# One-hots of the first block by a comparison on VectorE instead of three steps on ScalarE

## The reference, cut to what matters

```
scores = einsum('bshpd,hpnd->bshpn', q, sub_keys)
sv, si = top_k(scores, 16)                     # 16 best keys of each half
tv, tp = top_k(sv0 + sv1, 16)                  # 16 best of the 256 pairs
eidx   = si0 * 128 + si1                       # expert number, at tp
gw     = softmax(tv)
a      = gelu(einsum('td,ted->te', x, expert_u[eidx])) * gw
out    = einsum('te,ted->td', a, expert_v[eidx])
```

## Time and profile before

| | us |
|---|---|
| median of 3 runs (lowest, highest) | 3220.09 (3214.86, 3222.01) |
| the profiled execution | 3220.44 |
| its span | 3218.6 |
| VectorE busy in it | 2066.2 |
| TensorE matmuls busy | 2748.8 |
| ScalarE busy | 616.2 |
| DMA moved | 951.25 MB, mean 296 GB/s |

### The profile page before, as it was taken

The page is one execution under the profiler, slowest core; times in us unless marked ns, Lnnn a source line. Parts: engine busy times, 40 slices in busy tenths (PEclk is TensorE's granted clock), DMA queues, the critical chain, the costliest instruction groups (busy, mean ns, idle before and its releaser), DMA issues.

```text
span 3218.6 us, 31451 instructions
## 1 busy us (share of the span) xinstructions
PE 2748.8 (85%) x12106; PEld 2196.4 (68%) x12106; DVE 2066.2 (64%) x2764; ACT 616.2 (19%) x1230; POOL 912.3 (28%) x724
## 2 busy tenths in 40 slices
PE   5899889798999989989999999655657766999997
PEld 4688768587888868866888888554656665444443
DVE  6879675637355346822625116999999879656667
ACT  1011131020011010011110002011147778200000
POOL 0110001101010000000100002467776667656664
PEclk9999999899999989977999999877777776899998
DMA  9994359838885623321987446999999998999998
GB/s 363 390 399 137 104 188 380 358 131 345 355 357 221 254 86 128 106 68 39 393 324 307 148 158 270 391 367 415 421 421 410 387 388 266 351 401 414 415 413 354
DMA packets 149156, 951.25 MB, mean 296 GB/s; under 512 B 16560, under 2 KB 16560, under 8 KB 52400
## 3 DMA queue, kind: packets, MB, share of 16 engines
q0 software_dynamic: 103680, 620.80, 48.1%
q1 hardware_dynamic: 44208, 320.65, 26.3%
q10 hardware_dynamic: 1152, 8.26, 0.7%
HBM read 945.45 MB, written 4.19 MB: 295 GB/s over the span
## 4 chain that ended last, share of the span: by engine, by line
PE 42%; DVE 22%; DMA 21%; ACT 6%; issue 5%; POOL 4%; DVEq 0%; ACTq 0%; POOLq 0%
PE G L438 33%; DMA acc<-v_rows,proj 7%; DMA aring<-ada 7%; DVE aring L1276 3%; DVE vec L1868 3%; DMA mix<-v_rows,proj 3%; DVE aring L1840 2%; ACT vec L1139 2%; PE M L831 2%; DVE ring L1840 2%; DVE proj L1357 2%; DVE proj L1527 1%; POOL acc L426 1%; PE G L819 1%; DMA vec<-peer_u,proj 1%
## 5 line engine op out<-in xcount | busy, mean ns | idle before, releaser
L438 PE MATMUL G<-h,ring 128*128 128x256 f32 x4928 | 1081.9, 382 | 13.2 <-ACT h L915 13.2
L438 PEld LDWEIGHTS G<-h,ring 128*128 128x128 f32 x4928 | 942.9, 192 | 146.4 <-issue 16.5
L401 POOL DMA_DIRECT2D aring<-ada x208 | 109.8, 529 | 1633.7 <-DVE mods L1276 1626.4
L1276 DVE CUSTOM_DVE_ANT_0 aring<-aring,acc,vec 128x2048 f32<-128x2048 f32 x176 | 411.0, 2351 | 181.4 <-DMA aring<-ada 180.6
L438 PE MATMUL G<-proj,ring 128*128 128x256 f32 x2080 | 462.1, 386 | 10.6 <-DVE proj L1633 4.8
L438 PEld LDWEIGHTS G<-proj,ring 128*128 128x128 f32 x2080 | 403.0, 194 | 69.9 <-issue 12.8
L416 POOL DMA_INDIRECT aring<-peer_u,proj x128 | 217.5, 1700 | 348.6 <-DVE proj L1806 223.0
L872 PE MATMUL M<-sq,mix 128*128 128x512 f32 x688 | 301.5, 596 | 1.1 <-ACT mix L1153 1.1
L1840 DVE CUSTOM_DVE_ANT_0 aring<-sq,aring 128x2048 f32<-128x2048 f32 x108 | 245.4, 2291 | 27.6 <-DMA aring<-peer_u,proj 17.1
L1868 DVE SCALAR_TENSOR_TENSOR vec<-acc,dots,vec 128x1024 f32<-128x1024 f32 x149 | 191.2, 1283 | 100.9 <-DMA acc<-v_rows,proj 93.5
L883 ACT ACTIVATE proj<-G 128x256 f32 (+1 forms) x170 | 65.2, 383 | 979.2 <-PE G L438 979.1
(11 more groups left out here) (325 smaller groups left out, 2829.7 us busy)
## 6 DMA issues: line engine op xcount, KB each, us to landing
ring<-weights SPq DMA_DIRECT2D x219, 1024.0 KB, 5.0
aring<-ada POOLq DMA_DIRECT2D x208, 1024.0 KB, 12.2
sq<-v_blocks SPq DMA_DIRECT2D x43, 1024.0 KB
proj<-v_blocks SPq DMA_DIRECT2D x21, 1024.0 KB
ring<-first SPq DMA_DIRECT2D x16, 896.0 KB, 8.1
acc<-v_rows,proj POOLq DMA_INDIRECT x151
x<-xT SPq DMA_DIRECT2D x1, 2048.0 KB, 12.2
acc<-conds ACTq DMA_DIRECT2D x2, 1024.0 KB, 11.1
```

The costliest lines, as they stand in the source:

```text
L401: pool.dma_start(aring[:, n % SLOTS, :], ada[a]).then_inc(ada_in[n % SLOTS], 16)
L438: mm = nc.tensor.matmul(bank[:, 0:TOK], lhsT=ring[:, slot, weights_at + t * P:weights_at + (t + 1) * P], rhs=rhs[:, t, :], start=(t == 0), ...
L1276: V_.tensor_tensor_reduce(out=tile, in0=tile, in1=vector, scale=1.0, scalar=bias, op0=ALU.mult, op1=ALU.add, accum_out=column).then_inc(ad ...
```

## The change: what it does

The first block's one-hots are made as those of the second: one comparison on VectorE writes both `far` and `near` of a group (`one_hots(0, g)`), and ScalarE multiplies `far` by the coefficients (`weigh_hot(0, g)`). Abs and Relu on ScalarE go. VectorE's comparisons stand in its loop over the rows: behind row n (its dot, diagonal reading and selection part) come the groups of TensorE's row n + `MARK_AHEAD`; at n = 144 those of rows 144 and 149 both. A comparison of group g waits until group g-2 is spread (two buffers). `first_marked` tells ScalarE. TensorE's code is unchanged.

```diff
+MARK_AHEAD = 6
...
-            def one_hots(g):
-
-                if g >= 2:
-                    act.wait_ge(spread, g - 1)
-                both = hot[0][:, g % 2, :, :]
-                for s in range(2):
-                    for k in range(4):
-                        ins = nc.scalar.activation(both[:, s, k * P:(k + 1) * P], C("iota_keys"), ACT.Abs,
-                                                   bias=kept_idx(s, 4 * g + k), scale=-1.0)
-                ins.then_inc(hot_far, 1)
-                act.wait_ge(hot_far, g + 1)
-                b = both.rearrange("p s n -> p (s n)")
-                nc.scalar.activation(b, b, ACT.Relu, bias=ones[:, 0:1], scale=-1.0).then_inc(hot_near, 1)
-                act.wait_ge(hot_near, g + 1)
+            def weigh_hot(tk, g):
+
+                act.wait_ge(hot_marked if tk else first_marked, g + 1)
+                far = hot[tk][:, g % 2, 0, :]
                 for k in range(4):
...
                 if on_pe(n):
                     keep_row(n)
                     for g in spreads_after(n):
-                        one_hots(g)
+                        weigh_hot(0, g)
                         if g > 0:
                             keep_mix(0, g - 1)
...
-            def one_hots(g):
+            def one_hots(tk, g):
 
                 if g >= 2:
-                    dve.wait_ge(spread, P // 4 + g - 1)
+                    dve.wait_ge(spread, tk * (P // 4) + g - 1)
...
                 if n == NSLOT + SEL - 1:
                     coefficients(0)
+                    dve.wait_ge(turned_kept, 1)
+                for m in range(max(n + MARK_AHEAD, NSLOT + SEL) if n > NSLOT + SEL else NSLOT + SEL, n + MARK_AHEAD + 1):
+                    if n >= NSLOT + SEL and m < 2 * NSLOT and on_pe(m):
+                        for g in spreads_after(m):
+                            one_hots(0, g)
```

More of the change, by code:

```diff
@@ L333, in build @@
         turned, turned_kept = sem("turned"), sem("turned_kept")
-        hot_far, hot_near, hot0, hot1 = sem("hot_far"), sem("hot_near"), sem("hot0"), sem("hot1")
+        hot0, hot1 = sem("hot0"), sem("hot1")
         hot_marked = sem("hot_marked")
+        first_marked = sem("first_marked")
         spread, mix_in, block_used = sem("spread"), sem("mix_in"), sem("block_used")
@@ L1130, in keep_coefs @@
                 nc.scalar.activation(kept_coef[:, tk * P:(tk + 1) * P], G[1][:, 0:P], ACT.Copy).then_inc(turned_kept, 1)
-            def one_hots(g):
-                if g >= 2:
-                    act.wait_ge(spread, g - 1)
-                both = hot[0][:, g % 2, :, :]
-                for s in range(2):
-                    for k in range(4):
-                        ins = nc.scalar.activation(both[:, s, k * P:(k + 1) * P], C("iota_keys"), ACT.Abs,
-                                                   bias=kept_idx(s, 4 * g + k), scale=-1.0)
-                ins.then_inc(hot_far, 1)
-                act.wait_ge(hot_far, g + 1)
-                b = both.rearrange("p s n -> p (s n)")
-                nc.scalar.activation(b, b, ACT.Relu, bias=ones[:, 0:1], scale=-1.0).then_inc(hot_near, 1)
-                act.wait_ge(hot_near, g + 1)
+            def weigh_hot(tk, g):
+                act.wait_ge(hot_marked if tk else first_marked, g + 1)
+                far = hot[tk][:, g % 2, 0, :]
                 for k in range(4):
-                    ins = nc.scalar.activation(both[:, 0, k * P:(k + 1) * P], both[:, 0, k * P:(k + 1) * P], ACT.Copy,
-                                               scale=kept_coef[:, 4 * g + k:4 * g + k + 1])
-                ins.then_inc(hot0, 1)
+                    n = tk * P + 4 * g + k
+                    ins = nc.scalar.activation(far[:, k * P:(k + 1) * P], far[:, k * P:(k + 1) * P], ACT.Copy,
+                                               scale=kept_coef[:, n:n + 1])
+                ins.then_inc(hot1 if tk else hot0, 1)
             def keep_mix(tk, g):
@@ L1195, in _ @@
             keep_coefs(1)
[L1197 to L1205, removed]
             act.wait_ge(turned_kept, 4)
-            weigh_hot(0)
+            weigh_hot(1, 0)
             for g in range(P // 4):
                 if g + 1 < P // 4:
-                    weigh_hot(g + 1)
+                    weigh_hot(1, g + 1)
                 keep_mix(1, g)
@@ L1869, in v_add @@
                                             op1=ALU.add).then_inc(v_added, 1)
-            def one_hots(g):
+            def one_hots(tk, g):
                 if g >= 2:
-                    dve.wait_ge(spread, P // 4 + g - 1)
-                both = hot[1][:, g % 2, :, :].rearrange("p s (k n) -> p s k n", k=4)
-                where = kept[:, 256:512].rearrange("p (s n) -> p s n", s=2)[:, :, 4 * g:4 * g + 4]
+                    dve.wait_ge(spread, tk * (P // 4) + g - 1)
+                both = hot[tk][:, g % 2, :, :].rearrange("p s (k n) -> p s k n", k=4)
+                where = kept[:, 256 * tk:256 * tk + 256].rearrange("p (s n) -> p s n", s=2)[:, :, 4 * g:4 * g + 4]
                 keys_of_all = C("iota_keys").unsqueeze(1).unsqueeze(1).to_broadcast([P, 2, 4, P])
                 V_.tensor_tensor(both, keys_of_all, where.unsqueeze(3).to_broadcast([P, 2, 4, P]),
-                                 ALU.is_equal).then_inc(hot_marked, 1)
+                                 ALU.is_equal).then_inc(hot_marked if tk else first_marked, 1)
             for part in range(4):
@@ L1898, in _ @@
             for g in range(P // 4):
-                one_hots(g)
+                one_hots(1, g)
                 v_add(g)
```

## The result

The changed kernel takes 3261.8 us (median of 4, 3257.2 to 3266.4) against 3221.1 for the kernel before (median of 4): a ratio of 1.0129, 95% interval 1.0112 to 1.0146. Forecast were 3266 and a range of 3232 to 3284. The profiled execution after took 3266.3 us, its span is 3264.4.

What follows compares the result with a forecast made beforehand. VectorE got row 255 when the DMA delivered it; after the change VectorE was to be the bound. VectorE's work -0.6, waits +48.8, given back -2.9 made +45.3 us: 3266 us, range 3232 to 3284.

Steps and rivals of the forecast that it cites:

- VectorE's work of 294.4 us: Gathered rows 144 to 255 of the first retrieval: 257.9 us without waits before, plus 36.5 for 32 comparisons.
- ScalarE's removal at nothing: Taking Abs and Relu off ScalarE gains nothing, except the exponential's wait, 8.65 down to 1.7 us.
- The waits: VectorE's comparisons wait for TensorE's spread of two groups back: 48.8 us in all, 7.0 at row 144.
- the last three: Comparisons behind the selection, at rows 228, 233 and 238: waits of 5.1, 3.85 and 5.0 us, sum 13.95.
- d + 1.3: TensorE's chain from diagonal reading to spread released: its dot d, 5.9 us, plus start, spread and release; 7.2 us.
- lone-group key parts: Rows where VectorE has a key part of the selection and one group to mark: wait 3.15 us each.
- Given back later: Start of the second block's stretch: first v rows come early, so two waits of 2.9 us together go.
- The sum: Whole kernel: -0.6 + 48.8 - 2.9 = +45.3 us, giving 3266 us.
- The signs named: In the stretch: comparison waits of some 49 us, dots over 5 us, clock below 0.76, DMA share about 0.83.
- Warm TensorE: Rival: TensorE's dot stays at 3.84 us, so comparisons wait only 18.9 us; +15.4, 3236 us; chance 0.18.
- Marks truly ahead: Rival: the six rows' lead lets every comparison find its buffer free; -3.5 us, 3217 us; chance 0.06.
- Relief: Rival: with ScalarE relieved, rows come at the DMA's rate, 279 us, 16 us saved; 3204 us; chance 0.02.

Runs made afterwards that it cites:

- ahead2: The changed kernel with MARK_AHEAD 2 instead of 6, so each comparison stands four rows later on VectorE: 3218.7 us, ratio 0.9994.
- relief: The kernel before without the first block's Abs and Relu on ScalarE, no comparison on VectorE, mix wrong: 3201.7 us, ratio 0.9955.
- hybrid: The changed kernel with MARK_AHEAD 2, ten of 32 groups marked on VectorE, 22 on ScalarE by Abs and Relu: 3202.8 us, ratio 0.9951.

## Why the prediction was right, step by step

**VectorE's work of 294.4 us.** Right. ahead2, which has that work and no waits, took 294.6 us for it, and the run with twice the comparisons 38.2 more where 36.5 stood. One term in it, and in the 257.9 before, was too large: ScalarE's answer with the exponential, put at 1.7 us, was 0.4, since ScalarE, idle by then, had its table loaded long before VectorE asked. ScalarE's timeline in the changed kernel:

```profile
2624.04 1.28 ACT L1119 ACT_TABLE_LOAD   x1
2646.22 0.31 ACT L1119 ACTIVATE proj<-proj 128x128 f32<-128x128 f32 x1 [20.90 <-DVE proj L1798]
```

The load at 2624 is past, and the 0.31 us of the exponential are all that VectorE waits for. In the earlier trace rows ScalarE was behind, and load and exponential stood one after the other in VectorE's wait. The error is 1.3 us.

**ScalarE's removal at nothing.** Right within the stretch: relief shows that it is worth 14.5 us there while VectorE isn't loaded, ahead2 that VectorE's new work takes back exactly that. Behind the stretch it is not nothing; see below on what is given back.

**The waits.** The mechanism is the one that was forecast, place by place, and the total of 48.8 was 43.5. By its parts: at row 144 6.65 measured for 7.0; the last three 4.86, 3.06 and 5.44, together 13.4 for 13.95; the sixteen between 23.5 for 27.8. TensorE's dot, the term held for the least certain, was 6.0 us for 5.9. Two rows, of 5.21 and 6.60, had priced it; dots then ranged from 5.18 to 6.76, so that the mean of two came this close is in part luck. The mis-sized term is the rest of the chain, d + 1.3: in the rows at 2431 above, the comparison starts 7.59 us behind the dot's start where 6.66 + 1.16 + 0.05 = 7.87 was counted, since the spread's first matmul starts 0.16 before the dot's reported end and takes 1.06 for 1.16. That 0.28 us is too much in each of the 16. Against it d was 5.95 for 5.9 in them, so the chain was 7.02 for 7.20: 0.18 x 16 = 2.9 us. The other 1.5 is 0.1 us in each, nearly all of it because the view counts a wait from the reported end of the dot ahead (2.29 us) and the cover was counted with 2.21. Together that is the 4.3 missing, but for rounding. The pattern by parts holds less well than the sum: waits at the lone-group key parts were 3.59, 2.56, 3.47 and 2.12 us for 3.15; two of the waits forecast at 0.9 (rows 163 and 168) were too short for the view, as TensorE's dots ahead of them took 5.47 and 5.26.

**Given back later.** 4.3 us for 2.9 in the profiled execution, and the two waits of the earlier trace rows are gone, as was said. The reason stated, that VectorE is the bound, is not what does it: from the end of the last dot to the ninth v row's sum (`v_add`) it took 29.4 us before and 26.2 after, but 26.2 in relief and 26.3 in hybrid too, where VectorE still waits for gathered rows. Near the end of the stretch before, TensorE stood waiting for ScalarE's one-hots, and a gather stood behind TensorE (L416 a gather, L831 the transposes that free its slot):

```profile
2648.62 2.07 PE L819 MATMUL G<-vec 128*128 128x128 f32 x8 [3.76 <-ACT vec L1147]
2650.48 3.35 PE L831 MATMUL M<-cst,ring 128*128 128x128 f32 x16
...
2654.11 2.05 POOL L416 DMA_INDIRECT ring<-peer_u,proj  x1 [7.89 <-PE M L831]
```

The gathers of the v rows queue behind it: the first is issued 6.8 us before the end of the last dot, against 12.4 after the change and 16.3 in relief and hybrid. So these 3.2 us come from the relief of ScalarE, the term that was put at nothing. Where the other 1.1 comes from was not looked into. The tail before is from one execution; the tails of the other profiles lie between 541.6 and 544.6. The medians of ahead2 can't confirm the gain: 0.5 us less than before, interval 5.5 less to 1.6 more.

**The sum.** +45.3 forecast, +40 measured. VectorE's work against the time before: 0.0 in ahead2 (294.6 both, 0.8 of waits in it) for -0.6; of these 0.6, 0.4 is the end of the stretch before, read as 2671.4. The waits: 43.5 for 48.8. Both together: the stretch is 44.3 us longer for 48.2. It is 0.8 more than the waits: VectorE's time outside all listed waits is 295.0 us against 293.8 in ahead2, 1.2 more, since the view counts a wait only from the reported end of the instruction ahead, and ahead2 in turn has 0.4 of waits for rows. Given back: 4.3 for 2.9. 44.3 - 4.3 = 40.0, and the medians differ by 40.7.

**The signs named.** Waits before comparisons, long dots, no waits for rows, a clock of 0.75 for 0.76: all seen. The DMA share was to be 0.83 and is 0.92. The rate is what fell (348 of 421 GB/s, which is 0.83); for 118 MB instead of 117 the engines counted as busy 0.92 x 339 = 312 us instead of 0.98 x 295 = 289, so the busy share did not measure what they moved.

**The rivals.** Warm TensorE fell by the dots of 5.2 to 6.8 us. Marks truly ahead fell by 43.5 us of waits; it is what ahead2 does, and the time of 3217 stated for it was 3218.7 there. Relief fell by VectorE's work; its size was right for the case with VectorE's part left out: 3204 stated, 3201.7 measured, 14.5 us of it in the stretch for 16.

On the two rules of the Trainium skill: Perfetto Trace Analysis, Optimizing Scalar/DVE Operations, gave the direction, but saturation alone is not what made the change slower: ahead2 puts the same work on VectorE and takes no longer than the kernel before. The hybrid run adds that ten of the 32 groups moved that way are a gain where all of them are none: the 24 us of VectorE's waits in the earlier trace rows and the 8.65 of the earlier trace rows were room for it. The Trainium skill, TensorE: Matmul & The Clock Gate, Part 1, would have had the ramp left out; 11 to 16 us of waits hung on it here, because each slow dot stands in a chain in which VectorE waits. That is at most 0.5% of the span, so the figure of under 1% in that section of the Trainium skill is not contradicted, but it is a quarter to a third of the 43.5 us at stake.

## What to carry to other kernels

Work moved onto an engine is paid in two currencies: the engine's own slack in that stretch, and the new semaphore in front of it, which stalls everything queued behind. Count the slack as the length of the stretch less the engine's work from start to start (here 294.6 less 257.9, 37 us); the sum of its listed waits (32.5) falls short of it. "Made earlier" is not "ready earlier": six rows ahead the buffer was still in use in 20 of 30 cases, two rows ahead it had been free for 3.4 us or more. When neither engine can carry all of it, split it until the one resource that can't be moved (here the gathers, 280 us) is the bound.

## What the runs showed of the hardware that was not expected

The length of TensorE's pause alone does not tell how its next work runs: with six extra matmuls, a pause of 2.77 us was followed by a dot of 6.70 and one of 2.64 by a dot of 3.84, in the same loop. The changed kernel has such pairs too:

```profile
2461.77 5.26 PE L843 MATMUL B<-sq,acc 128*128 128x128 f32 x32 [6.42 <-DVE dots L1833]
...
2551.26 6.53 PE L843 MATMUL B<-sq,acc 128*128 128x128 f32 x32 [3.39 <-DVE dots L1833]
```

A pause of 6.42 us was followed by the shorter dot, one of 3.39 by the longer, and behind five pauses of 5.53 us the dots took 5.43, 5.61, 5.63, 5.72 and 6.53. What does set the single dot was not found; the mean over the 20 (6.0 us) was near the forecast.

GpSimd's gather issues took about 0.94 us beside VectorE's short selection steps or its waits, and mostly 1.9 to 2.8 us beside its dots. Of the 107 in the stretch of the changed kernel, 38 took under 1.1 us, and 36 of these overlapped a dot by 0.1 us at most; all 52 of 1.9 us or more overlapped dots by 0.9 us or more. That the dots cause it was not tested. Around 2432 us in the changed kernel:

```profile
2430.16 1.91 POOL L418 DMA_INDIRECT ring<-peer_u,proj  x1 [0.31 <-issue]
...
2432.37 0.94 POOL L418 DMA_INDIRECT ring<-peer_u,proj  x1 [0.30 <-issue]
```
